# Gate and up products of a SwiGLU feed-forward computed by feature instead of by token, in a two-layer decoder trunk

## The reference, cut to what matters

```python
def _swiglu(x, w_gate, w_up, w_down):
    return (jax.nn.silu(x @ w_gate) * (x @ w_up)) @ w_down
...
        h = _layernorm(ALPHA * h + mixed, ln1_w[layer], ln1_b[layer])
        h = _layernorm(ALPHA * h + _swiglu(h, ffn_w_gate[layer], ffn_w_up[layer], ffn_w_down[layer]),
                       ln2_w[layer], ln2_b[layer])
```

## Time and profile before

| | |
|---|---|
| median of 3 runs | 2483.06 us (2482.34 to 2483.46) |
| the profiled execution | 2483.77 us |
| its span, first to last instruction | 2481.8 us |
| TensorE busy | 2447.5 us, 99% of the span |
| weight loads (PEld), beside the matmuls | 2004.5 us, 81% |
| VectorE, ScalarE busy | 1409.1 us (57%), 1073.7 us (43%) |
| DMA | 440.88 MB, 178 GB/s |

### The profile page before, as it was taken

One profiled execution on the slowest core, in us unless ns is written; L12 is line 12 of the kernel. 1 busy time (PEld: TensorE's weight loads), 2 busy tenths in 40 slices (PEclk: granted clock), 3 DMA queues, 4 the chain that ended last, 5 costly groups with the idle time before them and its releaser, 6 DMA issues.

```text
span 2481.8 us, 39453 instructions
## 1 busy us (share of the span) xinstructions
PE 2447.5 (99%) x15550; PEld 2004.5 (81%) x15550; DVE 1409.1 (57%) x1743; ACT 1073.7 (43%) x1348; POOL 129.7 (5%) x172
## 2 busy tenths in 40 slices
PE   8999999999999999999999999999999999999997
PEld 6888788877888888888887788888788888888886
DVE  7788556676654454444446544666745444454445
ACT  4454355444444444443334344453544444443332
POOL 2000235420000000000000000000000000000000
PEclk9999999999999999999999999999999999999999
DMA  7556411255666666666565665455566666666554
GB/s 234 187 194 207 124 42 42 69 211 191 189 189 192 186 191 188 188 186 195 194 194 197 189 194 188 143 168 189 171 187 193 187 187 192 186 196 219 190 195 141
DMA packets 225884, 440.88 MB, mean 178 GB/s; under 512 B 13616, under 2 KB 24240, under 8 KB 224672
## 3 DMA queue, kind: packets, MB, share of 16 engines
q1 hardware_dynamic: 221760, 417.38, 54.4%
q0 software_dynamic: 3600, 21.55, 2.6%
q10 hardware_dynamic: 400, 0.18, 0.0%
HBM read 436.96 MB, written 2.10 MB: 177 GB/s over the span
## 4 chain that ended last, share of the span: by engine, by line
PE 93%; DVE 2%; DMA 2%; ACT 1%; issue 1%; POOL 0%; SPq 0%; DVEq 0%; ACTq 0%
PE ps L601 25%; PE ps L602 25%; PE ps L603 25%; PE ps L914 3%; PE ps L1099 1%; PE ps L797 1%; PE ps L807 1%; PE ps L1127 1%; PE ps L628 1%; PE ps L629 1%; PE ps L630 1%; PE ps L904 1%; DVE wlo L1712 1%; PE ps L858 1%; PE ps L762 1%
## 5 line engine op out<-in xcount | busy, mean ns | idle before, releaser
L1270 ACT CAST whi<-raw 128x1024 fp32r<-128x1024 f32 x735 | 772.5, 1052 | 1142.3 <-PE ps L603 1085.9
L1712 DVE TENSOR_TENSOR wlo<-raw,whi 128x1024 fp32r<-128x1024 f32 x549 | 669.9, 1224 | 620.6 <-ACT whi L1270 618.6
L601 PE MATMUL ps<-whi,ahi 128*128 128x512 f32 x2172 | 852.3, 392 | 2.7 <-DVE wlo L1712 2.7
L603 PE MATMUL ps<-whi,alo 128*128 128x512 f32 x2172 | 846.3, 390 | 0.0
L602 PE MATMUL ps<-wlo,ahi 128*128 128x512 f32 x2172 | 845.6, 389 | 0.0
L601 PEld LDWEIGHTS ps<-whi,ahi 128*128 128x128 f32 x2172 | 408.3, 188 | 88.0 <-DVE wlo L1712 3.6
L603 PEld LDWEIGHTS ps<-whi,alo 128*128 128x128 f32 x2172 | 408.0, 188 | 85.8
L602 PEld LDWEIGHTS ps<-wlo,ahi 128*128 128x128 f32 x2172 | 408.4, 188 | 84.0 <-issue 1.0
L2044 DVE TENSOR_TENSOR wlo<-raw,whi 128x1024 fp32r<-128x1024 f32 x193 | 236.1, 1224 | 249.5 <-ACT whi L1270 247.7
L601 PE MATMUL ps<-whi,hThi 128*128 128x512 f32 x656 | 255.4, 389 | 0.0
L603 PE MATMUL ps<-whi,hTlo 128*128 128x512 f32 x656 | 255.2, 389 | 0.0
(11 more groups left out here) (317 smaller groups left out, 1942.9 us busy)
## 6 DMA issues: line engine op xcount, KB each, us to landing
raw<-w_up SPq DMA_DIRECT2D x176, 512.0 KB, 3.6
raw<-w_down SPq DMA_DIRECT2D x176, 512.0 KB, 3.9
raw<-w_gate SPq DMA_DIRECT2D x170, 512.0 KB, 3.6
raw<-w_k SPq DMA_DIRECT2D x32, 512.0 KB, 4.0
raw<-w_r SPq DMA_DIRECT2D x32, 512.0 KB, 4.3
raw<-w_v SPq DMA_DIRECT2D x32, 512.0 KB, 3.6
raw<-w_o SPq DMA_DIRECT2D x32, 512.0 KB, 4.9
raw<-kv_v SPq DMA_DIRECT2D x32, 512.0 KB, 3.7
```

The source lines that it names most:

```text
L601: mm(o, hi[:, k, tok], whi[:, s, k2, :], start=(k == 0), stop=False)
L603: last = mm(o, lo[:, k, tok], whi[:, s, k2, :], start=False, stop=(k == kt - 1))
L1270: nc.scalar.copy(whi[:, s], src).then_inc(hi_done, 1)
L1712: V.tensor_tensor(wlo[:, s], src, whi[:, s].bitcast(F32), ALU.subtract).then_inc(split_done, 1)
```

## The change

In the gate and up jobs weights and activations change places. A 128x128 tile of the split weights becomes stationary and tokens stream, so that the result has features on the partitions. `ahi` and `alo` become the halves of one buffer `ahl`, so that one matmul of 512 columns streams the 256 high and the 256 low activations side by side over a tile of `whi`, and a second one of 256 columns streams the high activations over the tile of `wlo`. A job needs four banks: bank 4 * parity + f for feature block f, with high-by-high and low-weight sums in columns 0 to 255 and the low-activation sum in columns 256 to 511. The halves are added later: ScalarE copies the low half of the four banks to SBUF (`keep_lo`), VectorE adds the high half. In the first gate job (`narrow_chunk`), where banks 4 to 7 are taken by the layer norm's transposes, all three parts are matmuls of 256 columns into banks 0 and 1; its plain chunks use matmuls of 128 columns. The down product and every other stage keep their form. The transposes of the hidden block and their semaphore go.

```diff
-        ahi = sb("ahi", [P, KT, T], F32R)
-        alo = sb("alo", [P, KT, T], F32R)
+        ahl = sb("ahl", [P, 2, KT, T], F32R)
+        ahi, alo = ahl[:, 0], ahl[:, 1]
...
-        gtmp = carve(common, 32 * KB, TT, NB)
+        gtmp = carve(common, 32 * KB, FK, T)
+        low_half = carve(big, 80 * KB, FT, T)
...
+            def turned_chunk(c, ch, parity):
+
+                s = ch % RING
+                pe.wait_ge(split_done, c + (ch + 1))
+                for k2 in range(KC):
+                    k = ch * KC + k2
+                    for f in range(FK):
+                        o, cols = ps[:, 4 * parity + f, :], slice(f * P, (f + 1) * P)
+                        mm(o.rearrange("p (n t) -> p n t", n=2), whi[:, s, k2, cols], ahl[:, :, k, :], start=(k == 0), stop=False, skip_group_check=True)
+                        last = mm(o[:, 0:T], wlo[:, s, k2, cols], ahi[:, k, :], start=False, stop=(k == KT - 1), skip_group_check=True)
+                last.then_inc(chunk_used, 1)
+
+            def turned_job(c, u, parity):
+
+                pe.wait_ge(bank_free[parity], u + 1)
+                for ch in range(CJ):
+                    turned_chunk(c, ch, parity)
+
+            def narrow_chunk(c, ch):
...
+                    for f in range(FK):
+                        o, cols = ps[:, f // 2, (f % 2) * T:(f % 2 + 1) * T], slice(f * P, (f + 1) * P)
+                        mm(o, whi[:, s, k2, cols], ahi[:, k, :], start=False, stop=False, skip_group_check=True)
+                        mm(o, wlo[:, s, k2, cols], ahi[:, k, :], start=False, stop=False, skip_group_check=True)
+                        last = mm(o, whi[:, s, k2, cols], alo[:, k, :], start=False, stop=(k == KT - 1), skip_group_check=True)
...
-                        last = mm(ps[:, t, :], hF[:, k, tok], raw[:, ch, k2, :], start=(k == 0), stop=False)
+                        if by_feature:
+                            for f in range(FK):
+                                last = mm(ps[:, f // 2, (f % 2) * T + t * P:(f % 2) * T + (t + 1) * P], raw[:, ch, k2, f * P:(f + 1) * P], hF[:, k, tok],
+                                          start=(k == 0 and t == 0 and f % 2 == 0), stop=False, skip_group_check=True)
...
-                normed_job(2 * layer, f"up{layer}")
+                normed_job(2 * layer, f"up{layer}", True)
                 with pe.Fori(0, FB - 1) as i:
-                    job(i * (2 * CJ) + (c0 + 2 * CJ), i + (j0 // 2 + 1), 0, KT, ahi, alo)
-                    h_transposes(i + u0)
-                    job(i * (2 * CJ) + (c0 + 3 * CJ), i + (j0 // 2 + 1), 1, KT, ahi, alo)
-                    pe.wait_ge(hlo_done, i + (u0 + 1))
+                    turned_job(i * (2 * CJ) + (c0 + 2 * CJ), i + (j0 // 2 + 1), 0)
+                    turned_job(i * (2 * CJ) + (c0 + 3 * CJ), i + (j0 // 2 + 1), 1)
...
                     chunk(c, ch, 0, FT, hThi, hTlo)
-                    if ch == 1:
-                        h_transposes(u0 + FB - 1)
...
+                def keep_lo(c_end, parity, f0, kept):
+
+                    act.wait_ge(chunk_used, c_end)
+                    nc.scalar.copy(low_half[:, f0, :], ps[:, 4 * parity:4 * parity + FK, T:2 * T]).then_inc(kept, 1)
+
                 def hidden_hi(i, f0):
-                    act.wait_ge(h_tr, i + 1)
-                    A(hThi[:, f0, :], ps[:, 4:6, :].rearrange("p a (k t) -> p (a k) t", k=2), ACT.Copy).then_inc(hhi_done, 1)
+                    act.wait_ge(h_made, i + 1)
+                    nc.scalar.copy(hThi[:, f0, :], gtmp).then_inc(hhi_done, 1)
...
-                    split_hi(c + RING, u + 1, CJ)
-
-                    act.wait_ge(h_tr, i + (u0 + 1))
-                    act.wait_ge(chunk_used, c + CJ)
-                    A(gtmp, ps[:, 0:2, :], ACT.Silu).then_inc(bank_free[0], 1)
-                    hidden_hi(i + u0, bass.ds(i * 4, 4))
-                    split_hi(c + (RING + CJ), u + (1 + CJ // RING), CJ)
+                    keep_lo(c, 1, bass.ds(i * FK, FK), up_lo_kept)
+                    split_hi(c + RING, u + 1, 2)
+                    hidden_hi(i + u0, bass.ds(i * FK, FK))
+                    split_hi(c + RING, u + 1, CJ - 2, 2)
+                    keep_lo(c + CJ, 0, bass.ds(i * FK + FK, FK), gate_lo_kept)
+                    split_hi(c + (RING + CJ), u + (1 + CJ // RING), 2)
+                    act.wait_ge(bank_free[0], i + (j0 // 2 + 3))
+                    A(gtmp, gtmp, ACT.Silu).then_inc(silu_done, 1)
+                    split_hi(c + (RING + CJ), u + (1 + CJ // RING), CJ - 2, 2)
...
+                def multiply(i, f0, ups):
+
+                    low = low_half[:, f0, :]
+                    dve.wait_ge(up_lo_kept, i + 1)
+                    V.tensor_tensor(low, ps[:, 4:4 + FK, 0:T], low, ALU.add).then_inc(bank_free[1], 1)
+                    dve.wait_ge(bank_free[1], ups)
+                    dve.wait_ge(silu_done, i + 1)
+                    V.tensor_tensor(gtmp, gtmp, low, ALU.mult).then_inc(h_made, 1)
+
+                def gate_sum(i, f0):
+
+                    dve.wait_ge(gate_lo_kept, i + (layer * (FB - 1) + 1))
+                    dve.wait_ge(hlo_done, i + (u0 + 1))
+                    V.tensor_tensor(gtmp, ps[:, 0:FK, 0:T], low_half[:, f0, :], ALU.add).then_inc(bank_free[0], 1)
...
-                    multiply(c, i + (j0 // 2 + 2))
-                    split_lo(c + RING, CJ)
-                    hidden_lo(i + u0, bass.ds(i * 4, 4))
+                    multiply(i + u0, bass.ds(i * FK, FK), i + (j0 // 2 + 2))
+                    split_lo(c + RING, 2)
+                    hidden_lo(i + u0, bass.ds(i * FK, FK))
+                    split_lo(c + RING, CJ - 2, 0, 2)
+                    gate_sum(i, bass.ds(i * FK + FK, FK))
                     split_lo(c + (RING + CJ), CJ)
```

More of the change, by code:

```diff
@@ L329, in trunk @@
         xhat_done, ln_tr, ln_aff, ln_hi, h_done = (sem(n) for n in ("xhat_done", "ln_tr", "ln_aff", "ln_hi", "h_done"))
-        h_tr, hhi_done, hlo_done = (sem(n) for n in ("h_tr", "hhi_done", "hlo_done"))
+        gate_lo_kept, up_lo_kept, silu_done, h_made, hhi_done, hlo_done = (
+            sem(n) for n in ("gate_lo_kept", "up_lo_kept", "silu_done", "h_made", "hhi_done", "hlo_done"))
         qk_tr, qkt_set, s_made, nm_set, p_set, p_normed, pt_made, pt_set, o_made, o_kept, ohi_set, olo_set, s_read = (
@@ L1076, in _, with normed_job @@
             last_two(c + len(ZOUT), j + 2, KT, ahi, alo)
-            def normed_job(n, name):
+            def normed_job(n, name, by_feature):
                 c, j = PH[name]
@@ L1098, in plain @@
                         k = ch * KC + k2
-                        last = mm(ps[:, t, :], hF[:, k, tok], raw[:, ch, k2, :], start=(k == 0), stop=False)
+                        if by_feature:
+                            for f in range(FK):
+                                last = mm(ps[:, f // 2, (f % 2) * T + t * P:(f % 2) * T + (t + 1) * P], raw[:, ch, k2, f * P:(f + 1) * P], hF[:, k, tok],
+                                          start=(k == 0 and t == 0 and f % 2 == 0), stop=False, skip_group_check=True)
+                        else:
+                            last = mm(ps[:, t, :], hF[:, k, tok], raw[:, ch, k2, :], start=(k == 0), stop=False)
                     if t:
@@ L1113, in normed_job @@
                     pe.wait_ge(ln_hi, n * CJ + ch - PLAIN + 1)
-                    chunk(c, ch, 0, KT, ahi, alo)
+                    if by_feature:
+                        narrow_chunk(c, ch)
+                    else:
+                        chunk(c, ch, 0, KT, ahi, alo)
                 pe.wait_ge(ln_hi, (n + 1) * CJ)
-                job(c + CJ, j // 2, 1, KT, ahi, alo)
+                if by_feature:
+                    turned_job(c + CJ, j // 2, 1)
+                else:
+                    job(c + CJ, j // 2, 1, KT, ahi, alo)
             def ffn(layer):
@@ L1148, in _ @@
             ffn(0)
-            normed_job(1, "kvq")
+            normed_job(1, "kvq", False)
             jobs(PH["kvq"][0] + 2 * CJ, PH["kvq"][1] + 2, 6, KT, ahi, alo)
@@ L1257, in _, with split_hi @@
             A = nc.scalar.activation
-            def split_hi(c, u, n):
-                for ch in range(n):
+            def split_hi(c, u, n, at=0):
+                for ch in range(at, at + n):
                     s = (c + ch if isinstance(c, int) else ch) % RING
@@ L1567, in ffn @@
             def ffn(layer):
-                c0, _ = PH[f"up{layer}"]
+                c0, j0 = PH[f"up{layer}"]
                 u0 = layer * FB
+                def keep_lo(c_end, parity, f0, kept):
+                    act.wait_ge(chunk_used, c_end)
+                    nc.scalar.copy(low_half[:, f0, :], ps[:, 4 * parity:4 * parity + FK, T:2 * T]).then_inc(kept, 1)
                 def hidden_hi(i, f0):
-                    act.wait_ge(h_tr, i + 1)
-                    A(hThi[:, f0, :], ps[:, 4:6, :].rearrange("p a (k t) -> p (a k) t", k=2), ACT.Copy).then_inc(hhi_done, 1)
+                    act.wait_ge(h_made, i + 1)
```

(9 more changed lines are left out.)

22 lines of the change are left out of this document (6 added, 16 removed).

## The result

The changed kernel takes **2503.27 us** (median of 4 runs, 2502.16 to 2504.43); the kernel before, beside it, 2483.26 us. The ratio is 1.0082, with an interval from 1.0070 to 1.0093: 20 us slower. The forecast was 16 us faster, 2467.2 us. The full range that it named, 2451 to 2505 us, holds the result near its upper end; the forecast time and its direction are wrong.

What follows compares the result with a forecast made beforehand. The prediction took TensorE's matmul spacing to bound the kernel. Transposes -19.8, more and shorter matmuls +3.4, first gate job +0.3 and +0.2 summed to -15.9 us: 2467.2 us, full range 2451 to 2505.

Steps and rivals of the forecast that it cites:

- The bound: TensorE is 93% of the wait chain; in the feed-forwards time is the number of matmuls times their start spacing.
- The transposes: In the hidden block, 176 transposes in 22 blocks of 8 go, all on TensorE and the path: -19.8 us.
- more and shorter matmuls: In the turned chunks, 8 matmuls per row block instead of 6, same columns: 5.0 ns more, times 672, +3.4 us.
- So a full load can hide under 107 ns, though shown only for plain fp32.: In turned chunks, a full weight load fits beside a 256-column stream of 106.7 ns, so it adds nothing.
- The reasoning on the surcharge: On fp32r matmuls, 13.3 ns at 512 columns: 2.5 fixed, 10.8 growing with columns, so 114.6 ns at 256; chance 0.40.
- the first rival: Every fp32r matmul pays 13.3 ns whatever its length, 120.0 ns at 256 columns: 2483 us; chance 0.22.
- The sign taken from rows 11: ScalarE starts 0.43 us after a chunk's last matmul starts, with or without a load under it; called weak evidence.
- The slower rival: In turned chunks, alternating lengths hold matmuls at restart spacing, 231 and 124.4 ns: +24.4 us, 2507 us; chance 0.25.
- The first gate job: Narrow chunks with 256-column matmuls at 114.6 ns add 0.3 us; plain chunks at 109 add 0.2, or 0.5 at 112.
- The sum: Over the whole kernel, -19.8 + 3.4 + 0.3 + 0.2 = -15.9 us, giving 2467.2 us against the median.
- The load rule: A load takes its columns over 1.2, 107 ns for 128, leaving no slack beside a 256-column stream.

Runs made afterwards that it cites:

- half_load: The changed kernel with only the first 64 columns of each weight tile stationary in the turned jobs, half the features left out: 2466.25 us.
- the kernel wide: The changed kernel with the second matmul widened to 512 columns, adding the low by low product: 2770.10 us.
- grouped8: The changed kernel with matmuls reordered over each whole chunk, eight of 512 columns and then eight of 256: 2490.92 us.
- grouped4: The changed kernel with matmuls reordered per 128 rows of weight, four of 512 columns and then four of 256: 2494.92 us.
- before_cut: The kernel before with the third matmul of every triple cut into two of 256 columns in the 40 feed-forward loop jobs: 2502.40 us.

## Why the prediction was wrong, point by point

- **The bound** was read rightly: TensorE's spacing alone. No wait appeared, and two more operations a block on VectorE and ScalarE cost nothing.
- **The transposes** were worth what was counted (-19.8; 14.9 measured for seven of eight, interval up to 19.1).
- **The step that failed** is "more and shorter matmuls", +3.4 us. It measured (1413.3 - 1360.2) x 672 = **+35.7**. Two assumptions in it fell. The long matmuls were left at 226.7; they became 236.3, and that is 38 of the 53 ns. The short ones were put at 114.6 and took 117.0. Under both lies one sentence of the prediction: "So a full load can hide under 107 ns, though shown only for plain fp32." For fp32r a full tile is not free there: with it an even train takes 120.0 ns, with a tile of 64 columns 113.3. The doubt was written down and then not priced, because the rows in favour were clean.
- **The reasoning on the surcharge** was half right. It does grow with the columns, as taken from rows 11, but only where the tile is narrow: half_load, where the disturbance is gone, took 2466 us, 1 us from the forecast. With full tiles it is 13.3 at either length, as the first rival had it. The sign taken from rows 11, that a load under a matmul adds nothing, was read at matmuls of 512 columns. There it holds (226.7 in the kernel wide too), and it says nothing on 256.
- **The slower rival** gave 2507 for 2503 and named the right place, the restart's slow spacing that holds in the alternation. Its prices were the wrong way round: it had 231 for the long and 124.4 for the short matmul, where 236.3 and 117.0 came. It had 0.25 where the forecast had 0.40. The rows in its favour, 0.23 to 0.24 behind every interruption, were the only fp32r rows that showed an uneven train at all. They deserved more than rows of another type. That its total came within 4 us is in part luck, since the two wrong prices nearly cancel: 355.4 ns a pair against 353.3.
- **The first gate job** was put at +0.3 and +0.2. From the norm's first transpose to the first matmul of the up job it took 28.54 us before (600.60 to 629.14) and takes 29.73 after (604.51 to 634.24): +1.2 a layer, +2.4 in all, and the second layer gives the same. The narrow chunks run at 120.0 ns, 120 of them in place of 60 at 226.7: +0.8 a layer. The plain ones run at 111 to 112 ns and not at 109, near the 112 that stood as the other value: in each of two token tiles 48 matmuls take 5.6 us in place of 5.4, +0.4 a layer.
- **The sum** with measured terms: -19.8 + 35.7 + 2.4 = +18.3, against +20.0. The spans of the two profiled executions differ by 20.2; the 1.9 between is what the untouched stages differ by, +3.9 and -2.0.
- **The load rule.** The load alone, after a wait, occupied 109 ns in the earlier trace rows. The Trainium skill ("TensorE: Matmul & The Clock Gate", section LDWEIGHTS) makes a load last as long as its columns, 107 ns for 128; for 64 and 96 columns an estimate by that page is 53 and 80 ns. The runs agree so far that the loads' rows, 134, 161 and 188 ns for 64, 96 and 128 columns, are 27 ns apart. They show more than it states: between long matmuls, beside a short fp32r stream, even 96 columns cost the full step. For the gap of an isolated matmul the Trainium skill ("TensorE: Matmul & The Clock Gate", Back-to-back issue gap) has N / 2.4 + 2.5, 109 ns for 256; no even fp32r train here came below 113.3.

What stays open is why: whether the load or the width written to PSUM makes the short matmul dear, and why the long ones beside it slow down. Over a repeating pattern the spacings sum to 340.0, 346.7 or 353.3 ns a pair, and restarts run through much the same values (236, 228, 233, 231, 226.7) in grouped8 and grouped4 and, near 551 us, in the kernel before. That looks like two periodic streams falling into step. No run looked into it.

No version here that keeps all the work beats the kernel before. By the prices of the even trains a row block by feature costs 4 x (226.7 + 120.0) = 1387 ns with full tiles even without any alternation, 17.9 us over 672 row blocks, and the first gate jobs another 2.4: as much as the transposes give.

## What to carry to other kernels

A matmul's price is not its columns alone. Here an fp32r matmul of 256 columns with a 128-column tile took 120.0 ns and not the half of 226.7, and between long ones it raised these to 236.3. Before work is cut into shorter matmuls, price the short one by a row of the same type and in the same mixture; an even train of another type says little. If lengths must be mixed, the order matters, so try some: grouping eight by eight gave back 11 (by the casts) to 12 of the 20 us lost, and the cut triples of before_cut lost less per row block than either grouping, though with the old operands.

## What the runs showed of the hardware

- fp32r matmuls in an even train: 226.7 ns for 512 columns, 120.0 for 256 with a full tile, 113.3 for 256 with 64 stationary columns.
- After a group of short matmuls (grouped8), long ones are 233, 236, 228, 233, 231 ns apart before they return to 226.7. A restart after a wait near 551 us of the kernel before went 240, 235, 233, 236, 224, 231, 236, 228, 233, 230 first.
- In the alternation 64, 72, 96 and 128 stationary columns give 340.0, 346.7, 353.3 and 353.3 ns a pair; the output then has as many partitions as the tile has columns.
- A bf16 matmul of 256 columns between fp32r ones of 512 makes the pair 358 ns, though its load's row is 95 ns long and not 188.
- The same 512 columns streamed from two places 16 KB apart, into four banks in turn, keep 226.7 ns.
